# Differential attention kernel: the head's output turned by VectorE in squares of 32x32 instead of by TensorE, its pair stored as one tile in four pieces, the gate's loads issued by ScalarE

## The reference

```python
    def block(args):
        qb, start = args
        sc = jnp.einsum('bqhmd,bkhmd->bhmqk', qb, k).astype(f32) * scale
        q_chunk = (start + jnp.arange(Q_BLOCK)) // CHUNK
        mask = key_chunk[None, :] <= q_chunk[:, None]
        p = jax.nn.softmax(jnp.where(mask[None, None, None], sc, NEG_INF), axis=-1)
        attn = p[:, :, 0] - lam * p[:, :, 1]
        return jnp.einsum('bhqk,bkhd->bqhd', attn.astype(v.dtype), v)

    starts = jnp.arange(s // Q_BLOCK) * Q_BLOCK
    o = from_blocks(lax.map(block, (to_blocks(q, Q_BLOCK), starts)))
    o = rms_norm(o, subln_g) * (1.0 - lambda_init)
    o = o.reshape(b, s, BRANCH) * jax.nn.silu(z)
    return o @ w_out
```

## Time and profile before

| | |
|---|---|
| median of 3 runs | 1906.76 us (1906.63 to 1907.32) |
| the profiled execution | 1907.34 us, its span 1905.5 us |
| PE busy | 1866.0 us, 98% |
| VectorE (DVE) busy | 1379.5 us, 72% |
| ScalarE (ACT) busy | 810.1 us, 43% |
| GpSimd (POOL) busy | 794.4 us, 42% |
| DMA packets, share of 16 engines | 394048, 473.16 MB, 76.4% in the main queue |
| granted TensorE clock | 1.00 throughout |

### The profile page before, as it was taken

The page is one execution under the profiler, slowest core; times in us unless marked ns, Lnnn a source line. Parts: engine busy times, 40 slices in busy tenths (PEclk is TensorE's granted clock), DMA queues, the critical chain, the costliest instruction groups (busy, mean ns, idle before and its releaser), DMA issues.

```text
span 1905.5 us, 26384 instructions
## 1 busy us (share of the span) xinstructions
PE 1866.0 (98%) x9072; PEld 1540.9 (81%) x9072; DVE 1379.5 (72%) x2028; ACT 810.1 (43%) x1516; POOL 794.4 (42%) x844
## 2 busy tenths in 40 slices
PE   4999999999999999999999999999999999999998
PEld 1488888888888888888888888888888888888886
DVE  3687888886655546787887877878778776569467
ACT  5633333333444433444443444444444445546452
POOL 2076565655644523344344434434443422116023
PEclk9999999999999999999999999999999999999999
DMA  9898898886674698786877778686777679657777
GB/s 354 253 313 279 274 297 278 284 290 232 214 267 160 237 356 263 225 250 192 253 229 227 235 216 252 198 254 212 232 240 221 213 228 291 207 186 257 258 240 265
DMA packets 394048, 473.16 MB, mean 248 GB/s; under 512 B 22614, under 2 KB 268476, under 8 KB 391228
## 3 DMA queue, kind: packets, MB, share of 16 engines
q1 hardware_dynamic: 393632, 471.43, 76.4%
q10 hardware_dynamic: 284, 0.05, 0.0%
HBM read 323.54 MB, written 147.86 MB: 247 GB/s over the span
## 4 chain that ended last, share of the span: by engine, by line
PE 93%; DVE 1%; DMA 1%; ACT 0%; issue 0%; SPq 0%; POOL 0%; DVEq 0%; POOLq 0%; ACTq 0%
PE ps L1752 30%; PE ps L1754 30%; PE ps L1753 30%; PE ps L1885 2%; PE ps L1861 1%; PE ps L1904 1%; PE ps L1721 0%; DMA ubf<-s_dr 0%; DMA z_dr<-cc 0%; PE ps L1833 0%; DVE ring L1310 0%; ACT h L1040 0%; DVE xt L1632 0%; DVE tB L1330 0%; DVE tB L1327 0%
## 5 line engine op out<-in xcount | busy, mean ns | idle before, releaser
L1752 PE MATMUL ps<-blk,ring 128*128 128x512 f32 x1524 | 603.3, 396 | 2.6 <-DVE blk L1357 1.9
L1754 PE MATMUL ps<-blk,ring 128*128 128x512 f32 x1524 | 594.6, 390 | 0.0
L1753 PE MATMUL ps<-blk,ring 128*128 128x512 f32 x1524 | 594.2, 390 | 0.0
L1752 PEld LDWEIGHTS ps<-blk,ring 128*128 128x128 f32 x1524 | 286.3, 188 | 66.0 <-issue 9.7
L1754 PEld LDWEIGHTS ps<-blk,ring 128*128 128x128 f32 x1524 | 286.0, 188 | 60.8
L1753 PEld LDWEIGHTS ps<-blk,ring 128*128 128x128 f32 x1524 | 286.5, 188 | 55.8
L1310 DVE TENSOR_TENSOR ring<-sums,ring 128x512 fp32r<-128x512 f32 x256 | 234.7, 917 | 95.5 <-ACT ring L1006 93.6
L836 POOL TENSOR_TENSOR sums<-raw 128x512 f32<-128x512 f32 x128 | 191.5, 1496 | 226.9 <-DVE ring L1310 206.0
L1006 ACT ACTIVATE ring<-sums 128x512 fp32r<-128x512 f32 x256 | 160.6, 628 | 179.3 <-PE ps L1754 175.6
L1310 DVE TENSOR_TENSOR ring<-raw,ring 128x512 fp32r<-128x512 f32 x192 | 179.2, 934 | 58.9 <-ACT ring L1006 58.5
L836 POOL TENSOR_TENSOR sums<-sums,raw 128x512 f32<-128x512 f32 x128 | 190.2, 1486 | 20.8 <-DVE ring L1310 14.3
(11 more groups left out here) (159 smaller groups left out, 3181.7 us busy)
## 6 DMA issues: line engine op xcount, KB each, us to landing
raw<-in_diff_w_in_dram SPq DMA_DIRECT2D x64, 1024.0 KB, 7.8
d_dr<-cc SPq DMA_DIRECT2D x124, 256.0 KB, 3.2
cc<-d_dr SPq DMA_DIRECT2D x124, 256.0 KB, 4.1
ubf<-s_dr SPq DMA_DIRECT2D x113, 256.0 KB, 5.0
ada<-in_ada_w_dram SPq DMA_DIRECT2D x88, 256.0 KB, 7.3
tb<-in_diff_w_out_dram SPq DMA_DIRECT2D x32, 512.0 KB, 5.5
t_dr<-tb SPq DMA_DIRECT2D x32, 512.0 KB, 4.9
ada<-in_ada_w_dram SPq DMA_DIRECT2D x32, 512.0 KB
```

The lines of the kernel that those rows point to most:

```text
L1752: MM(dst, a_hi, b_hi, start=start, stop=False, skip_group_check=True)
L1753: MM(dst, a_hi, b_lo, start=False, stop=False, skip_group_check=True)
L1754: return MM(dst, a_lo, b_hi, start=False, stop=stop, skip_group_check=True)
```

## The change

`o_turn` is gone from TensorE's list. VectorE turns `o_sb` itself, with one instruction that turns each square of 32x32 in place, and the product with the gate follows as one instruction over both halves. Since only squares are turned, the four squares of a row of squares are still in the wrong places; the transfers put that right: the gate is loaded in four pieces of 32 partitions in the same order of squares, and the store writes each square to its place in `s_dr`. In both, one run in HBM is 32 numbers, 128 B. `ozf` and `osum` become one tile `o_all` of 8 x 128 numbers per partition, stored in four pieces of 32 partitions. The norm's weight now runs along the free axis: `sub_row`, loaded once as a row and broadcast, goes into `out_scale`, and `sub8` is gone.

The order on SP changes too. In odd iterations, from a = 3 on, the pair before is stored: two pieces ahead of the first slot and two ahead of the second. `load_v` moves from the head of the iteration to behind its first slot. For heads 0 to 6 `load_z` is issued by ScalarE, behind the slots and ahead of `square`; for head 7 it stays on SP, with four transfers, and `store_pair` issues all four pieces at once.

```diff
+SIDE = 32
...
-        ozf = at("ozf", [P, 2, 2, P], F32, z_at)
-        osum = at("osum", [P, 4, P], F32, z_at)
+        o_all = at("o_all", [P, 8, P], F32, z_at)
+        ozf, osum = o_all[:, 0:4].rearrange("p (t m) n -> p t m n", t=2), o_all[:, 4:8]
...
-        s_dr = dram("s_dr", [8, HEADS, P, PAIRS, P])
+        s_dr = dram("s_dr", [HEADS, 8 * P, PAIRS, P])
...
+        PAIR_STORED = 16 * (P // SIDE)
...
-                sp.dma_start(z_sb[:, :, :],
-                             z_dr[h * 2:h * 2 + 2, :, qb * P:(qb + 1) * P].rearrange("m p n -> p m n")).then_inc(z_ld, 16)
-
-            def store_pair(h, p):
+                for c in range(0, P, SIDE):
+                    sp.dma_start(z_sb[c:c + SIDE].rearrange("j m (b i) -> j (m b) i", i=SIDE),
+                                 z_dr[h * 2:h * 2 + 2, :, qb * P + c:qb * P + c + SIDE].rearrange(
+                                     "m (b j) i -> j (m b) i", j=SIDE)).then_inc(z_ld, 16)
+
+            def store_pair(h, p, pieces=range(0, P, SIDE)):
 
                 sp.wait_ge(ozf_ok, h * NB + 2 * p + 2)
-                sp.dma_start(s_dr[0:4, h, :, p].rearrange("o p n -> p o n"),
-                             ozf.rearrange("p i m n -> p (i m) n")).then_inc(s_st, 16)
                 sp.wait_ge(osum_ok, 4 * (h * PAIRS + p + 1))
-                sp.dma_start(s_dr[4:8, h, :, p].rearrange("o p n -> p o n"), osum[:, :, :]).then_inc(s_st, 16)
+                for c in pieces:
+                    sp.dma_start(s_dr[h, :, p, c:c + SIDE].rearrange("(o j) i -> j o i", j=SIDE),
+                                 o_all[c:c + SIDE].rearrange("j o (b i) -> j (o b) i", i=SIDE)).then_inc(s_st, 16)
...
-                sp.wait_ge(s_st, 32 * PAIRS * (h + 1))
-                sp.dma_start(ubf[k][:, 1, 1], s_dr[s, h].rearrange("p t n -> p (t n)")).then_inc(unit_in[k], 16)
+                sp.wait_ge(s_st, PAIR_STORED * PAIRS * (h + 1))
+                sp.dma_start(ubf[k][:, 1, 1], s_dr[h, s * P:(s + 1) * P].rearrange("p t n -> p (t n)")).then_inc(unit_in[k], 16)
...
+                if n == NA + 12:
+                    sp.dma_start(sub_row[:, :], subln[None, :].to_broadcast([P, VD])).then_inc(sub_in, 16)
...
                     a = (h - 1) * NB + qb
-                    load_v(h - 1, qb)
                     load_qk(*divmod(a + 1, NB))
-                    for _ in range(sum(SPREAD[qb])):
+                    for k in range(sum(SPREAD[qb])):
+                        if a > 1 and a % 2 and k < 2:
+                            store_pair((a - 2) // NB, (a - 2) % NB // 2, (0, SIDE) if k == 0 else (2 * SIDE, 3 * SIDE))
                         slot(n)
                         n += 1
+                        if k == 0:
+                            load_v(h - 1, qb)
...
-                    load_z(h - 1, qb)
-                    if a and a % 2 == 0:
-                        store_pair((a - 1) // NB, (a - 1) % NB // 2)
...
@@ ScalarE @@
+            def load_z(h, qb):
+
+                a = h * NB + qb
+                if qb == 0:
+                    for e in range(4):
+                        act.wait_ge(stored[e], (h * 4 + 4) * 32)
+                if a > 0:
+                    act.wait_ge(ozf_ok, a)
+                for c in range(0, P, SIDE):
+                    act.dma_start(z_sb[c:c + SIDE].rearrange("j m (b i) -> j (m b) i", i=SIDE),
+                                  z_dr[h * 2:h * 2 + 2, :, qb * P + c:qb * P + c + SIDE].rearrange(
+                                      "m (b j) i -> j (m b) i", j=SIDE)).then_inc(z_ld, 16)
...
+                    load_z(h - 1, qb)
                     if a + 1 == LH * NB:
                         unit_high(0)
                     square(h - 1, qb)
...
@@ VectorE @@
-                V.tensor_scalar(o_sb[:, :], ps[:, OB, 0:VD], ofac[:, 0:1], None, ALU.mult).then_inc(o_ok, 1)
+                else:
+                    dve.wait_ge(cols_ok, 2)
+                STT(o_sb[:, :], ps[:, OB, 0:VD], ofac[:, 0:1], sub_row[:, :], ALU.mult, ALU.mult).then_inc(o_ok, 1)
 
             def gate(h, qb):
 
                 a = h * NB + qb
+                dve.wait_ge(o_ok, a + 1)
+                V.transpose(ps[:, OB, VD:2 * VD], o_sb[:, :]).then_inc(oT_done, 1)
+                dve.wait_ge(z_ld, (a + 1) * 16 * (P // SIDE))
+                if a > 1:
+                    dve.wait_ge(s_st, PAIR_STORED * (a // 2))
                 dve.wait_ge(oT_done, a + 1)
-                dve.wait_ge(z_ld, (a + 1) * 16)
-                if a > 1:
-                    dve.wait_ge(s_st, 32 * (a // 2))
-                for m in range(2):
-                    i = STT(ozf[:, a % 2, m], ps[:, OB, VD + m * P:VD + (m + 1) * P], sub8[:, m:m + 1],
-                            z_sb[:, m], ALU.mult, ALU.mult)
-                i.then_inc(ozf_ok, 1)
+                TTV(ozf[:, a % 2], ps[:, OB, VD:2 * VD].rearrange("p (m n) -> p m n", m=2), z_sb[:, :, :],
+                    ALU.mult).then_inc(ozf_ok, 1)
...
@@ TensorE @@
-                    if a:
-                        o_turn(*before(a))
...
-                o_turn(*((LH, qb - 1) if qb else (LH - 1, NB - 1)))
...
-            o_turn(LH, NB - 1)
```

More of the change, by code:

```diff
@@ L150, in build @@
         gpT = at("gpT", [P, P], F32)
-        sub8 = at("sub8", [P, 2], F32)
         lamp = at("lamp", [P, 2], F32)
@@ L232, in build @@
         ofac = at("ofac", [P, 1], F32, z_at)
+        sub_row = at("sub_row", [P, VD], F32, z_at)
         BLK = 2 * KB * HALF * 4
@@ L280, in build @@
         lam_p, lam_mm, lam_e, lam_ok = sem("lam_p"), sem("lam_mm"), sem("lam_e"), sem("lam_ok")
-        c_e, c_ok = sem("c_e"), sem("c_ok")
+        c_ok, sub_in = sem("c_ok"), sem("sub_in")
         x_sq, x_ss, x_ms, x_rs, x_sc = sem("x_sq"), sem("x_ss"), sem("x_ms"), sem("x_rs"), sem("x_sc")
@@ L1009, in _ @@
             act.wait_ge(c_in, 16)
-            A(cexp[:, :], craw[:, :], ACT.Exp, scale=-1.0).then_inc(c_e, 1)
+            A(cexp[:, :], craw[:, :], ACT.Exp, scale=-1.0).then_inc(c_ok, 1)
             for t in range(TT):
@@ L1282, in _ @@
             V.memset(yss[:, :, :, :], D * EPS).then_inc(yss_c, 1)
-            dve.wait_ge(c_e, 1)
+            dve.wait_ge(c_ok, 2)
             V.tensor_scalar(cexp[:, :], cexp[:, :], 1.0, None, ALU.add).then_inc(c_ok, 1)
-            dve.wait_ge(c_ok, 2)
+            dve.wait_ge(c_ok, 3)
             V.reciprocal(cexp[:, :], cexp[:, :]).then_inc(c_ok, 1)
-            dve.wait_ge(c_ok, 3)
+            dve.wait_ge(c_ok, 4)
             TTV(cact[:, :], craw[:, :], cexp[:, :], ALU.mult).then_inc(c_ok, 1)
@@ L1294, in _ @@
             TTV(lamp[:, 1:2], cols[:, R_LAM + 2:R_LAM + 3], cols[:, R_LAM + 3:R_LAM + 4], ALU.mult).then_inc(lam_p, 1)
-            V.tensor_scalar(sub8[:, :], cols[:, R_SUB:R_SUB + 2], (1.0 - LAMBDA_INIT) / 2, None, ALU.mult).then_inc(cols_ok, 1)
             dve.wait_ge(lam_e, 1)
@@ L1557, in _ @@
                 take(n)
+            dve.wait_ge(sub_in, 16)
+            V.tensor_scalar(sub_row[:, :], sub_row[:, :], (1.0 - LAMBDA_INIT) / 2, None, ALU.mult).then_inc(cols_ok, 1)
             n = NA + PARTS_IN * NP
@@ L1727, in ada_rows @@
                 if s == 0:
-                    pe.wait_ge(c_ok, 4)
+                    pe.wait_ge(c_ok, 5)
                 pe.wait_ge(*ada_landed(s))
@@ L1898, in weighted @@
                 last.then_inc(pv_done, 1)
-            def o_turn(h, qb):
-                a = h * NB + qb
-                pe.wait_ge(o_ok, a + 1)
-                for m in range(2):
-                    last = TR(ps[:, OB, VD + m * P:VD + (m + 1) * P], o_sb[:, m * P:(m + 1) * P], ident[:, :])
-                last.then_inc(oT_done, 1)
-            def before(a):
-                return divmod(a - 1, NB)
             for n in range(NA, NA + PARTS_IN * NP):
```

## The result

The changed kernel takes 1962.96 us (median of 4 runs, 1957.02 to 1967.26), the kernel before 1907.04 in the same comparison: a ratio of 1.029, 95% interval 1.0262 to 1.0317. It is 56 us slower, where 21 were forecast; the range, 1896 to 1990, held it.

A forecast was written before the change was run, and what follows sets the result against it. TensorE was taken as the bound (busy 98% of the span, 93% of the last chain). Terms -14.1 + 22.6 + 8.4 + 2.0 + 2.5 = +21.4 us gave 1928 us by the median, range 1896 to 1990.

The forecast's parts named there:

- it lands at 1269.2: Block 3: the last store piece lands then, from the cc load landing at 1265.0 plus 4.2 us of new transfers.
- Stall 3.2 us, in seven heads 22.6: Block 3: the gate product waits for the stores, so aT_low reaches TensorE 3.2 us late, 22.6 us in all.
- Blocks 5 and 7 hidden: Blocks 5 and 7: the stores' delay costs TensorE nothing; in block 7 aT_low ends 1221.3, needed at 1221.5.
- The last head, 4.5: Last head: 2.0 us for the gate's load behind four stores, 2.5 us for the last pair's store.
- 13.0 ns: DMA price of one 128 B packet, on a straight line between 10.6 ns (64 B) and 27.3 ns (512 B).
- Rival 4: A 128 B packet costs no less than one of 512 B, 27.3 ns: all odd blocks stall, 2028 us; chance 0.15.
- the turn on VectorE: Per block, one turn in squares and one 128x256 product, 0.41 us each, 0.82 in place of 0.60.
- 14.1 us less: TensorE: 64 times two turns of o_sb go, 0.22 us for each two.
- ScalarE takes over four issues (about 1.5 us): ScalarE issues the gate's loads before square, whose 3 us wait for TensorE hides them: no cost.
- Rival 3: Odd blocks: the late gate delays ScalarE's issues, square and exps by 0.8 us, 11 us more, 1940; chance 0.08.
- 2.5 us come through whole: End of attention: last pair stored at once, 3.3 us of packets where 0.87 remained, TensorE already waiting: 2.5 us.
- 1.2 us, in seven heads 8.4: Block 1: aT_low ends at 1245.0, TensorE needs it at 1243.8; a stall of 1.2 us, 8.4 in all.

The follow-up runs named there:

- act_mid: Changed kernel with a pair's four small-packet stores issued by ScalarE in odd iterations, before aT_high, in place of SP: 2113.88 us, 1.1084.
- late_4: Kernel before, with only aT_low of block 3 repeated 4 times in heads 0 to 6, so TensorE's product with v_sb comes late: 1934.29 us, 1.0138.
- late_6: Kernel before, with only aT_low of block 3 repeated 6 times in heads 0 to 6: 1949.94 us, 1.022.
- split_behind: gate_behind with two store pieces at the even iteration's end, two in the odd one behind the first slot's transfers and v load: 1920.92 us, 1.007.
- turn_behind: Kernel before's transfers, VectorE turning into SBUF, gate product behind aT_low, first store waiting for ozf alone; squares not put in place: 1896.62 us, 0.9947.
- z_sp: Changed kernel with the gate's four loads issued by SP again, behind the iteration's slots, in place of ScalarE: 1954.72 us, 1.0253.
- gate_behind: Changed kernel with VectorE turning into SBUF (osq) and the gate product, which waits for the stores, moved behind aT_low: 1938.28 us, 1.0166.
- four_ahead: Changed kernel with all four stores of a pair ahead of the first slot in odd iterations: 1961.28 us, 1.0279.
- even_end: Changed kernel with the four stores of a pair issued at the end of the even iteration again, packets still 128 B: 1933.17 us, 1.0139.

## Why the prediction was off by size

**Right.** The sign, and the mechanism with its places. The last piece of block 3, "it lands at 1269.2", 10.6 us behind the q load's issue: over seven heads the last piece landed 11.2 behind it. "Stall 3.2 us, in seven heads 22.6": 3.6, 25.2. Blocks 5 and 7 hidden: blocks 5 without a gap, blocks 7 too, but one. The last head, 4.5: 6.2.

**Right, the packets.** "13.0 ns" for one of 128 B. The gate's loads on ScalarE's queue give 2.5% of 16 x 1965.5 us over 61212 packets [the page above], 12.8 ns. In act_mid the stores are on that queue as well:

```profile
q10 hardware_dynamic: 173532, 21.57, 6.7%
```

The added 112320 packets cost 6.7% of 16 x 2110.8 us less those 786 us, that is 13.1 ns each. Rival 4 is refuted by this: stores of 128 B run at the price of loads. The Trainium skill, "DMA: Bandwidth & Descriptors", Specifications, says that below 512 B the engine reads, modifies and writes; no cost of that shows here.

**Right, the turn on VectorE.** 0.41 us taken, 448 ns measured into PSUM and 434 into SBUF. The estimate from the Trainium skill's "VectorE: DVE Perf Modes", the three transpose paths, 0.62, was further off.

**The step that failed** is one the sum did not have: every stall was priced at its own length ("Stall 3.2 us, in seven heads 22.6"). Behind a gap like that TensorE ran at half clock, and 18.3 us were lost, nearly half of the miss of 38.6; late_4 and late_6 show it with nothing of the change in the program. With the gaps of block 3 gone, the clock came back too: split_behind lost 1.7 us to it, behind a gap of 1.8 us in the last head.

Of the rest, 14.6 us are gaps that the sum had at nothing or too short (blocks 2, 3, 4, 6 and 7, and the last head; see the table), and 5.7 are left over, 3 to 4 of them because the turns taken from TensorE were worth 10 to 11 us and not "14.1 us less" (turn_behind).

**Smaller steps that failed.** "ScalarE takes over four issues (about 1.5 us) [...] `square` sat waiting 3 us for TensorE each time, which hides them": in block 1 it waited 2.3 us, the issues begin only when the gate's product is through, and giving the issues back to SP took 8 us off (z_sp against the changed kernel). Rival 3 had that mechanism, but behind all four odd blocks and at 11 us. It shows behind block 1 alone (`square` comes 1.0 to 1.8 us into block 2 in six heads, with 4.7 us of gaps) and in block 1, which follows an even one; it does not take the forecast's place, it adds to it. Block 7 was worked out as "hidden": so it is in six heads, not in head 6, where four loads of the output projection's units stand between the two halves of the stores:

```profile
1593.15 0.46 SPq L714 DMA_DIRECT2D ubf<-in_diff_w_out_dram  x1
...
1593.65 0.43 SPq L720 DMA_DIRECT2D ubf<-s_dr  x1
...
1594.13 0.43 SPq L714 DMA_DIRECT2D ubf<-in_diff_w_out_dram  x1
...
1594.60 0.43 SPq L720 DMA_DIRECT2D ubf<-s_dr  x1
...
1595.13 1.57 SPq L578 DMA_DIRECT2D s_dr<-o_all  x2
...
1603.02 0.42 DVE L1552 TENSOR_TENSOR o_all<-ps,z_sb 128x256 f32<-128x256 f32 x1 [5.40 <-DMA s_dr<-o_all]
...
1604.19 0.55 PE L1776 MATMUL ps<-v_sb,aT_hi 128*128 128x256 f32 x1 [4.05 <-DVE aT_lo L1570]
```

The one block was taken for all seven, without a look at the place where the list differs. And the end of the last head, "2.5 us come through whole", was a gap of 2.8 and the half clock behind it:

```profile
1762.95 0.50 PE L1776 MATMUL ps<-ub 128*128 128x512 f32 x1 [2.81 <-DVE ub L1613]
```

**Right by luck.** Block 1, "1.2 us, in seven heads 8.4", measured 8.5; but only 3.4 us of them are the forecast wait for aT_lo. The other 5.2 stand before the turn of `prob` and go when SP issues the gate's loads (z_sp).

In block 3 two errors cancelled. The working took the cc load to land as before, 6.4 us behind the q load's issue, and put 4.2 us of transfers behind it. It landed 9.0 us behind, since the first two pieces stand ahead of it in SP's list, and the last piece followed 2.2 us later. That VectorE is held up by the late cc load as well was not in it: this makes 1.5 of the 3.6 us by itself (gate_behind), and with all four pieces ahead of the load the whole stall (four_ahead).

## What to carry to other kernels

Price a new gap of the engine that bounds the kernel with what its clock does behind it, from a run that makes just such a gap if no trace has one. Where a wait has two late releasers, the profile names only the last: curing that one shows what the other would have cost, and here the transfer that merely stood behind the new ones in SP's list was good for 1.5 of 3.6 us. When a product is moved out of the way, look at what else waits for its buffer: here `square` did. Taking work off the busiest engine paid 10 us at the most here, and every microsecond of it could be lost again by where four small transfers stand in a queue.

## What was not expected of the hardware

- A gap of 2.6 us on TensorE, seven times, was followed by half clock each time (12.6 us lost in all), one of 4.0 us by no more (11.9). In even_end gaps of 1.6 to 3.0 us in block 3 were followed by none, and in gate_behind one of 1.8 us in block 1 was. The length alone does not decide it; what does, these runs leave open.
- An issue is not a fixed price. A store of 32 partitions in 128 B runs took SP 0.32 us to issue at the least, 0.56 in the median and 2.0 at the most in the changed kernel, and the issues behind it grew as well (1.7 us for a `v_dr` store in the timeline above). With ScalarE issuing such stores while SP issued others, four took 5.8 us, and in act_mid they landed 6.2 us after their issue in the median, where the changed kernel had 3.8.
